# A recurrence split by token halves: its first half in steps beside the projections of the second half, the attention after them

## The chip, the cores and the metric

The kernel runs on one NeuronCore of a Trainium2 chip. TensorE (PE) does the matmuls, VectorE (DVE) and ScalarE (ACT) the elementwise work, GpSimd (POOL) a little of it; SyncE (SP) and POOL issue transfers. Each engine works through its own program in order, and they meet through semaphores. The metric is the device time of one execution in microseconds. The kernel before took 3598.67 us (median of three runs, 3595.58 to 3598.70).

## The reference, cut to what matters

Two transformer-like blocks over 1024 tokens of width 1024, in float32. The change lies in the mixer of the second block:

```python
h = _rmsnorm(x, mix_norm_gain[l])
proj = h @ w_in[l]
p_rwkv, p_attn = proj[..., :RWKV_COLS], proj[..., RWKV_COLS:]
y_rwkv = _rwkv7_mixer(p_rwkv, ...)
q, k, v = (t.reshape(B, S, ATTN_HEADS, HEAD_DIM) for t in jnp.split(p_attn, 3, axis=-1))
q = _partial_rotary(q, positions); k = _partial_rotary(k, positions)
o = _dilated_attention(q, k, v)
x = x + jnp.concatenate([y_rwkv, y_attn], axis=-1) @ w_out[l]
```

`_rwkv7_mixer` shifts each projection by a token, computes decay, gates and keys per token, and runs a recurrence of a 64x64 state over the tokens, eight heads wide:

```python
def step(state, inp):
    r_t, w_t, k_t, v_t, kk_t, a_t = inp
    sa = jnp.einsum('bhvk,bhk->bhv', state, -kk_t)
    state = (state * w_t[:, :, None, :]
             + sa[..., None] * (kk_t * a_t)[:, :, None, :]
             + v_t[..., None] * k_t[:, :, None, :])
    y = jnp.einsum('bhvk,bhk->bhv', state, r_t)
    return state, y
```

The attention has eight heads of width 64 too; each query sees earlier keys through three dilated windows.

## The kernel before, in words

Matmuls of weights are done three times (high by high, high by low, low by high part of the float32 numbers): `dense` (line 297) runs one weight tile of 128 output channels, 8 slices of the inner dimension, 24 matmuls of 512 columns for one half of the tokens. ACT makes the high part `w_hi` of a weight tile, DVE the low part `w_lo`, two tiles ahead (`next_tile`).

**Projections of block two** (`in3_*`, from line 1954). 26 tiles in the list `IN3` for the first 512 tokens, then the same 26 for the last 512: `wa2` and `gd2` (low-rank inputs of decay, a and gate), 12 `rkv`, 12 `aqkv` (the attention's q, k, v). ACT copies each result from PSUM, DVE does the token shift (two instructions, "mix") or the rotary turn (three), and SP writes the tile to DRAM (`K.rkv`, `K.attn`).

**Heads.** Then three streams share the engines: two of the recurrence (`rwkv_*`, g = 0 and 1) and the attention (`attention_*`). Each stream is a Python generator that yields at the end of a step; `braid` takes one step of each stream in turn, and writes them one behind the other into each engine's program. The second recurrence stream starts at step 20 (`LAG`). A recurrence stream has four units u (two pairs of heads j, two token halves hf), in the order `halves(g)`: (2g, 0), (2g, 1), (2g+1, 0), (2g+1, 1). Counting the yields, a unit has 56 steps for hf = 0 and 55 for hf = 1. In a unit: gates and decay (light on PE), products of 64x64 blocks, five levels of a triangular inverse (`Y`, then `X` and `Xt`, with a DVE step between), a chain `S` of up to 8 small steps for the state, and the norm. The attention has four blocks j of two heads, 40 steps each. In one there are 16 units (8 query blocks i by 2 heads): scores on PE, mask and maximum on DVE (`add_min`), exp on ACT, transposes on PE, copy on ACT, values on PE, copy on ACT; then a norm over the block. `half_over` makes each engine of a stream wait for the end of the stream's unit before.

All engines wait at `in3_over` before the heads: every tile of the projections is done and written. When the heads are over, the output projection `out2` (tiles `X2HA`, `X2LA`, ...) begins.

**Order of the work.** There is a second way of mixing here, used elsewhere in this kernel: a `Lane` keeps a list `bg` of generators, and `slots(n)` in the main program adds `fine` to an account for each slot and takes a step of the first generator when it has reached 1. A `dense` tile with one token half has 8 slots on PE, one behind each of its 8 slices (3 matmuls); DVE and ACT take the 8 slots in one go at the start of the tile, behind the split of a later weight and ahead of the wait for the tile's own result.

**Memory.** The streams use PSUM banks 0 and 1, 2 and 3 and (attention) 4 to 7; the projections use 0 to 3, the rotary turn 4 to 7. In the trace `r_...` are tiles of the recurrence (`r_in` its loaded r, k, v), `a_...` those of the attention, `XHB` and `XLB` the normalised input of the second token half, `over1hB` and `over1lB` the places that hold projected tiles until they are written.

## Time and profile before

| | |
|---|---|
| median of three runs | 3598.67 us (3595.58 to 3598.70) |
| the profiled execution | 3591.73 us, span 3589.9 us, granted clock 0.953 |
| PE busy over the span | 3265.2 us (91%) |
| DVE, ACT, POOL busy | 1751.6, 1188.3, 250.0 us (49%, 33%, 7%) |
| chain that ended last | PE 74%, DVE 15%, ACT 6%, issue 3% |
| second token half's projections | from 1928 to 2077 us |
| heads | from 2086 to 2758 us; `out2` from 2760.6 us |

"Granted clock" is the share of 2.4 GHz that the throttle gave TensorE on average over a stretch; it has two levels, 1.2 and 2.4 GHz. In the waits view a line says who waited for whom, the microseconds in total, the number of times and the longest. In the time-ordered view a row has its start, its length, engine, line, operation, output <- inputs, the number of instructions merged, and in brackets the idle time before it with what ended it.

### The profile page before, as it was taken

Reading aid. Unit: us, or ns where it says so; the run is one execution under the profiler, and the core shown is the slowest. Engines: PE = TensorE matmul, PEld = TensorE weight load, DVE = VectorE, ACT = ScalarE, POOL = GpSimd, SP = SyncE. Lnnn points to the kernel's source line nnn. Section 1 sums busy time; section 2 is a strip of 40 time slices with the busy share of each in tenths; the row PEclk is TensorE's granted clock in tenths of the full one; section 3 lists DMA queues with packets and bytes.
Section 4 is the critical chain, followed back from the end, with each engine's and each line's share of the span. In section 5 each row is a group of like instructions: output and inputs, shape, how many; then the busy total and the mean of one; then the engine's idle time right before and its main releaser. Section 6 shows DMA issues by size and latency. Waiting matters only on the chain.

```text
span 3589.9 us, 55150 instructions
## 1 busy us (share of the span) xinstructions
PE 3265.2 (91%) x23686; PEld 2733.8 (76%) x23686; DVE 1751.6 (49%) x2928; ACT 1188.3 (33%) x2050; POOL 250.0 (7%) x210
## 2 busy tenths in 40 slices
PE   5999878889989999998999978887877999999998
PEld 4887767768878888887777857675756878888887
DVE  6646343346574243436654444455555553333355
ACT  4231354452453221223433233433322431212133
POOL 1111010011130000001210000000001000000000
PEclk8999899999999999999999979898989999999999
DMA  2111121114332111123443410101001222111123
GB/s 100 67 65 48 63 81 66 69 58 141 135 108 90 55 42 53 40 77 102 140 150 135 156 52 20 37 2 36 2 19 60 94 96 69 47 47 49 48 93 111
DMA packets 86770, 262.28 MB, mean 73 GB/s; under 512 B 10208, under 2 KB 10336, under 8 KB 86400
## 3 DMA queue, kind: packets, MB, share of 16 engines
q1 hardware_dynamic: 76512, 224.07, 18.5%
q0 software_dynamic: 5120, 16.86, 1.3%
q10 hardware_dynamic: 4896, 17.84, 1.2%
q8 instruction: 187, 3.06, 0.4%
q14 instruction: 55, 0.45, 0.0%
HBM read 216.51 MB, written 42.21 MB: 72 GB/s over the span
## 4 chain that ended last, share of the span: by engine, by line
PE 74%; DVE 15%; ACT 6%; issue 3%; DMA 1%; POOL 1%; ACTq 0%; SPq 0%; DVEq 0%; POOLq 0%
PE ps L125 71%; PE ps L128 2%; DVE m_S L169 1%; DVE w_lo L159 1%; ACT w_hi L156 1%; ACT L138 1%; DVE r_t L159 1%; DVE HB L169 1%; PE ps L124 1%; DVE r_in L159 1%; DVE HB L159 1%; ACT m_D L138 1%; DVE r_Xa L159 1%; DVE r_t L169 0%; ACT r_t L138 0%
## 5 line engine op out<-in xcount | busy, mean ns | idle before, releaser
L159 DVE TENSOR_TENSOR w_lo<-w_raw,w_hi 128x1024 fp32r<-128x1024 f32 (+3 forms) x353 | 397.4, 1128 | 360.0 <-ACT w_hi L156 356.4
L125 PE MATMUL ps<-XHA,w_hi 128*128 128x264 f32 (+3 forms) x1456 | 476.4, 327 | 32.0 <-ACT m_G L138 8.8
L125 PE MATMUL ps<-XLA,w_hi 128*128 128x264 f32 (+3 forms) x1456 | 464.7, 319 | 0.0
L125 PE MATMUL ps<-XHA,w_lo 128*128 128x264 f32 (+3 forms) x1456 | 462.8, 318 | 0.0
L156 ACT ACTIVATE w_hi<-w_raw 128x1024 fp32r<-128x1024 f32 (+3 forms) x353 | 340.1, 964 | 348.0 <-PE ps L125 281.3
L125 PE MATMUL ps<-XHB,w_hi 128*128 128x512 f32 x920 | 369.2, 401 | 7.8 <-POOL XLB L159 5.7
L125 PE MATMUL ps<-XLB,w_hi 128*128 128x512 f32 x920 | 361.0, 392 | 0.0
L125 PE MATMUL ps<-XHB,w_lo 128*128 128x512 f32 x920 | 360.6, 392 | 0.0
L125 PEld LDWEIGHTS ps<-XHA,w_hi 128*128 128x128 f32 x1456 | 282.8, 194 | 64.5 <-issue 25.5
L125 PEld LDWEIGHTS ps<-XLA,w_hi 128*128 128x128 f32 x1456 | 283.3, 195 | 21.8 <-issue 4.1
L125 PEld LDWEIGHTS ps<-XHA,w_lo 128*128 128x128 f32 x1456 | 283.3, 195 | 16.7
L125 PEld LDWEIGHTS ps<-XHB,w_hi 128*128 128x128 f32 x920 | 174.5, 190 | 50.0 <-issue 9.3
L125 PEld LDWEIGHTS ps<-XLB,w_hi 128*128 128x128 f32 x920 | 174.4, 190 | 37.8 <-issue 3.1
L125 PEld LDWEIGHTS ps<-XHB,w_lo 128*128 128x128 f32 x920 | 174.1, 189 | 37.1
L159 DVE TENSOR_TENSOR HB<-HB,ps 128x512 f32<-128x512 f32 (+1 forms) x136 | 88.2, 655 | 217.8 <-PE ps L125 217.5
L125 PE MATMUL ps<-X2HA,w_hi 128*128 128x512 f32 x416 | 164.3, 395 | 9.3 <-DVE X2LA L159 5.2
L125 PE MATMUL ps<-X2LA,w_hi 128*128 128x512 f32 x416 | 163.5, 393 | 0.0
L125 PE MATMUL ps<-X2HA,w_lo 128*128 128x512 f32 x416 | 163.2, 392 | 0.0
L125 PE MATMUL ps<-X2HB,w_hi 128*128 128x512 f32 x416 | 162.7, 391 | 0.0
L125 PE MATMUL ps<-X2HB,w_lo 128*128 128x512 f32 x416 | 161.9, 389 | 0.0
L125 PE MATMUL ps<-X2LB,w_hi 128*128 128x512 f32 x416 | 161.8, 389 | 0.0
L166 DVE TENSOR_SCALAR C<-G,vecs 128x512 f32<-128x512 f32 x88 | 51.0, 579 | 214.8 <-ACT G L156 214.8
(445 smaller groups left out, 6244.7 us busy)
## 6 DMA issues: line engine op xcount, KB each, us to landing
w_raw<-in_f_gate SPq DMA_DIRECT2D x66, 512.0 KB, 3.2
w_raw<-in_f_up SPq DMA_DIRECT2D x66, 512.0 KB, 3.2
w_raw<-in_w_out SPq DMA_DIRECT2D x32, 512.0 KB, 3.2
w_raw<-in_f_down SPq DMA_DIRECT2D x48, 320.0 KB, 2.9
w_raw<-in_f_down SPq DMA_DIRECT2D x32, 384.0 KB, 3.1
w_raw<-in_w_rkv SPq DMA_DIRECT2D x24, 512.0 KB, 3.3
w_raw<-in_w_attn SPq DMA_DIRECT2D x24, 512.0 KB, 3.3
w_raw<-in_w_qkvo SPq DMA_DIRECT2D x16, 512.0 KB, 3.3
```

Source lines behind the costliest of these rows:

```text
L124: return Issued(e.matmul(out, a, b, start=start, stop=stop, skip_group_check=True))
L125: return Issued(e.matmul(out, a, b, start=start, stop=stop))
L128: return Issued(self.eng and self.eng.transpose(out, src, ident))
L138: return Issued(self.eng and self.eng.activation(out, src, func, **kw))
L156: return Issued(self.eng and self.eng.activation(out, src, ACT.Copy))
L159: return Issued(self.eng and self.eng.tensor_tensor(out, a, b, op))
L166: return Issued(self.eng.tensor_scalar(out, a, s1, s2, op0, op1))
L169: return Issued(self.eng and self.eng.scalar_tensor_tensor(out=out, in0=a, scalar=s, in1=b, op0=op0, op1=op1))
```

## The change

The order of a stream's units becomes (2g, 0), (2g+1, 0), (2g+1, 1), (2g, 1), so that the first two units of each stream need the first token half alone. The two recurrence streams begin with the first tile of the second token half's projections (`BEGIN`), in the background list, with `fine` = 0.55: 26 tiles x 8 slots x 0.55 give 114 steps there, of which the first 6 (`BEG`) are empty. What is left of them is run with the attention (`heads_rest`), which joins the braid when the projections are over and begins with two empty steps (`ATT`).

What goes with it: the state after the first half of a stream's first unit is kept aside (`D.kept`, one DVE copy) until its last unit; the second half's projections use PSUM banks 4 and 5, their rotary turn 6 and 7; their spill buffers and the low-rank inputs move into parts of `HB`; the loads `r_in<-rkv` move from SP's queue to POOL's, which has its own order of the two streams (`rwkv_load` in `rwkv_pool`); SP's queue holds the loads of the attention alone after the projections, and the first attention block's load, before issued while the projections ran (`LATER`), now comes behind `in3_over`; PE waits before `BEGIN` until DVE has read the last rotary result. The rotary turn of a tile stands one tile later in DVE's text, behind a further weight split.

```diff
+BESIDE, BEG, ATT = 0.55, 6, 2
...
-        b = K.fg.take(P, (name, m, c))
+        b = (ring or K.fg).take(P, (name, m, c))
...
-EARLY, LATER = (1, "rkv", 6), (1, "aqkv", 8)
+EARLY, BEGIN = (0, "aqkv", 4), (1, "wa2", 0)
...
+def banks3(K, c):
+    return K.fh if c else K.fg
...
+def lora_place(K, c, rows):
+
+    if c:
+        return K.HB[rows, 0 if rows.stop <= 64 else 2, 512:1024]
+    return K.HB[rows, 4 if rows.stop <= 64 else 5, 0:512]
...
     for c, name, i in IN3:
-        dense(P, K, S, name, i, 8, K.X, ready, [WIDE3[c]], [c])
+        if (c, name, i) == BEGIN:
+            P.wait_ge(S.dve, ("rot", 0, 10))
+            heads_begin(P, K, rwkv_pe)
+        dense(P, K, S, name, i, 8, K.X, ready, [WIDE3[c]], [c], banks3(K, c))
...
+        if t == BEGIN:
+            heads_begin(A, K, rwkv_act)
...
+            V.tt(K.ident2[:, :], K.ident[:, 0:64], K.ident[:, 64:128], ADD).then_inc(K.c.dve, "ident2")
+            heads_begin(V, K, rwkv_dve)
...
-            D.dma(K.amask[:, :], K.I["a_mask"]).then_inc(K.a_mask, by=16)
-            for g in range(2):
-                for n in range(3):
-                    at = SPILL3[0, "rkv", 6 * g + n]
-                    D.wait_ge(K.pst[at % 4], ("out", at))
-                rwkv_load(D, K, g, 0)
-        if t == LATER:
-            for n in range(3):
-                at = SPILL3[1, "aqkv", n]
-                D.wait_ge(K.pst[at % 4], ("out", at))
-            attention_load(D, K, 0)
...
-    return [(2 * g, 0), (2 * g, 1), (2 * g + 1, 0), (2 * g + 1, 1)]
+
+    return [(2 * g, 0), (2 * g + 1, 0), (2 * g + 1, 1), (2 * g, 1)]
+
+
+def first_half_over(L, K):
+
+    n3_over(L, K)
+    for sig in K.hs:
+        L.wait_ge(sig, ("h2", 1))
+    L.wait_ge(K.in3.pe, ("aqkv", 11, 0))
+    L.wait_ge(K.in3.act, ("aqkv", 0, 11))
+    L.wait_ge(K.in3.dve, ("turned", 0, 10))
+    for n in range(20, 24):
+        L.wait_ge(K.pst[n % 4], ("out", n))
...
+    yield from pause(BEG)
+    P.wait_ge(K.in3.act, ("aqkv", 0, 11))
...
+        elif u == 2:
+            V.vcopy(x.S0[:, 0:64], x.S0[:, 512:576]).then_inc(d, ("S", u, 0))
         else:
-            V.vcopy(x.S0[:, 0:64], x.S0[:, 512:576]).then_inc(d, ("S", u, 0))
+            V.vcopy(a16(x.S0[:, 0:64]), D.kept).then_inc(d, ("S", u, 0))
...
+        if u == 0:
+            V.after(d)
+            V.vcopy(D.kept, a16(x.S0[:, 512:576])).then_inc(d)
...
+        if u == 3:
+            V.wait_ge(K.rws[1 - g].pe, ("g", 3) if g else ("a", 3))
...
+        if u:
+            rwkv_load(G, K, g, u)
...
 def rwkv_load(D, K, g, u):
     T, (j, hf) = K.rw[g], halves(g)[u]
     for n in range(3):
+        at = SPILL3[hf, "rkv", 3 * j + n]
+        D.wait_ge(K.pst[at % 4], ("out", at))
+    for n in range(3):
         D.dma(T.in3[:, n, :], K.rkv[4 * n + j][:, 512 * hf:512 * hf + 512]).then_inc(T.ld, ("in", u), by=16)
-
-
-def rwkv_sp(D, K, g):
-    T, S = K.rw[g], K.rws[g]
-    for u in range(4):
-        half_over(D, S, u, None)
-        if u:
-            rwkv_load(D, K, g, u)
-        yield from pause(58)
...
 def attention_sp(D, K):
     S = K.at
+    in3_over(D, K)
+    D.dma(K.amask[:, :], K.I["a_mask"]).then_inc(K.a_mask, by=16)
     for j in range(4):
         if j:
+            D.wait_ge(K.a_ld, ("in", j - 1))
             D.wait_ge(S.pe, ("w", j - 1, 15))
-            attention_load(D, K, j)
-        yield
-        yield
-        yield from pause(34)
-        yield from pause(2 + Q5)
-        yield
+        attention_load(D, K, j)
 
 
...
 def attention_pe(P, K):
     S, ps = K.at, K.atb
+    yield from pause(ATT)
+    in3_over(P, K)
...
+        yield
+
+
+def heads_begin(L, K, rwkv):
+
+    L.drain()
+    L.streams = [rwkv(L, K, 0), rwkv(L, K, 1)]
+    L.bg.append(braid(L.streams))
+    L.fine = BESIDE
+
+
+def heads_rest(L, attention):
+
+    L.streams.append(attention)
+    L.drain()
+    L.fine = 0
 
 
 def heads_pe(P, K):
-    in3_over(P, K)
-    braid([rwkv_pe(P, K, 0), rwkv_pe(P, K, 1), attention_pe(P, K)])
+    heads_rest(P, attention_pe(P, K))
...
+    for g in range(2):
+        rwkv_load(G, K, g, 0)
+    first_half_over(G, K)
+    G.bg.append(braid([rwkv_pool(G, K, 0), rwkv_pool(G, K, 1)]))
+    G.drain()
 
 
 def heads_sp(D, K):
-    in3_over(D, K)
-    braid([rwkv_sp(D, K, 0), rwkv_sp(D, K, 1), attention_sp(D, K)])
+    attention_sp(D, K)
...
+    K.fh, K.sr = Banks(ps[4:6]), Banks(ps[6:8])
...
+        K.pS2 = [K.HB[:, 6 + n // 2, 512 * (n % 2):512 * (n % 2) + 512] for n in range(4)]
...
     in3_pe(P, K)
-    P.drain()
-    P.fine = 0
     heads_pe(P, K)
```

Three places in the order of the instructions. **PE, in a tile of the second token half's projections.** Before, the tile's matmuls stand next to each other, with a rotary matmul (`over1lB,cst`) between two tiles:

```order
L125 MATMUL ps<-XHB,w_lo 128x512
L125 MATMUL ps<-over1lB,cst 128x512
L125 MATMUL ps<-XHB,w_hi 128x512
L125 MATMUL ps<-XLB,w_hi 128x512
L125 MATMUL ps<-XHB,w_lo 128x512
```

Now, with stream 0 in its state chain (`r_S,r_Xa`) and stream 1 in a level of its inverse (`r_Xa,r_GB`):

```order
L127 MATMUL ps<-XHB,w_hi 128x512
L127 MATMUL ps<-XLB,w_hi 128x512
L127 MATMUL ps<-XHB,w_lo 128x512
L127 MATMUL ps<-r_S,r_Xa 64x64 x2
L127 MATMUL ps<-XHB,w_hi 128x512
L127 MATMUL ps<-XLB,w_hi 128x512
L127 MATMUL ps<-XHB,w_lo 128x512
L127 MATMUL ps<-r_S,r_Xa 64x64 x2
L127 MATMUL ps<-r_Xa,r_GB 64x64 x16
```

One slice or two of the tile stand between two steps of the recurrence. Of the recurrence's 4016 matmuls in the program, 1814 now stand among the tiles, and 2202 behind the last tile.

**DVE, over a tile in the same place.** Before, a weight split, two instructions of token shift, the next split:

```order
L159 TENSOR_TENSOR w_lo<-w_raw,w_hi 128x1024
L159 TENSOR_TENSOR over1hB<-over1hB 128x512
L169 SCALAR_TENSOR_TENSOR over1hB<-over1hB,vecs 128x512
L159 TENSOR_TENSOR w_lo<-w_raw,w_hi 128x1024
L159 TENSOR_TENSOR over1hB<-over1hB 128x512
```

Now the shift (`HB<-p_G`, then `HB<-HB,vecs,p_G`) and the split stand together, and the steps behind them until the next tile's:

```order
L161 TENSOR_TENSOR r_Xa<-r_Xa,ps 128x512
L161 TENSOR_TENSOR r_in<-r_in,ps 128x512
L161 TENSOR_TENSOR HB<-p_G 128x512
L171 SCALAR_TENSOR_TENSOR HB<-HB,vecs,p_G 128x512
L161 TENSOR_TENSOR w_lo<-w_raw,w_hi 128x1024
L161 TENSOR_TENSOR r_S<-ps,r_t 128x64
L161 TENSOR_TENSOR r_t<-ps,cst 128x512
L161 TENSOR_TENSOR r_S<-ps,r_t 128x64 x2
```

So three DVE instructions of a tile, the first of which waits for the tile's end on PE and its copy on ACT, stand between two steps of the recurrence.

**PE, at the end of the heads.** Before, the recurrence is last, and the output projection follows its last matmul:

```order
L125 MATMUL ps<-r_t,r_S 64x64
L125 MATMUL ps<-r_t,cst 128x512 x2
L125 MATMUL ps<-r_GD,r_gl 128x512
L125 MATMUL ps<-X2HA,w_hi 128x512
L125 MATMUL ps<-X2LA,w_hi 128x512
```

Now the recurrence's last matmul (`HB,r_gl`) stands early in the attention's last block:

```order
L127 MATMUL ps<-a_k,a_q 128x384 x2
L127 MATMUL ps<-HB,r_gl 128x512
L130 MATMUL ps<-cst,a_A 128x128 x3
L127 MATMUL ps<-a_VT,a_PT 128x64 x2
L130 MATMUL ps<-cst,a_A 128x128 x3
L127 MATMUL ps<-a_VT,a_PT 128x64 x3
L127 MATMUL ps<-a_k,a_q 128x512 x2
```

Behind it stand 68 of that block's 72 value matmuls (`a_VT,a_PT`), its norm, and then `out2`, with nothing of another stream between them.

## Rows read from the trace of the kernel before

**Rows 1.** Busy time by stretch; first line names the columns.
```profile
core 0: us, PE busy (x) PEld busy (x) DVE busy (x) ACT busy (x) POOL busy (x), PEclk, DMA share, GB/s
1928.00:2077.00 149.00, 149.00 (x642) 120.19 (x640) 65.97 (x79) 48.72 (x73) 0.00 (x0) 1.00 0.46 162
...
2086.00:2760.00 674.00, 546.50 (x9152) 449.44 (x9150) 338.38 (x665) 223.59 (x481) 25.70 (x16) 0.88 0.05 16
2592.00:2732.00 140.00, 107.45 (x2268) 87.78 (x2263) 71.62 (x122) 30.50 (x48) 6.67 (x4) 0.88 0.04 13
```

**Rows 2.** Waits, 2592 to 2732: us, times, longest.
```profile
PE ps L125 <- DVE r_in L159: 13.0, 9, 3.6
```

**Rows 3.** PE in order of time: stream starts, ends of attention blocks, next stage.
```profile
2085.65 2.07 PE L125 MATMUL ps<-r_WA,r_wl 32*128 32x512 f32 x4 [8.46 <-issue]
...
2204.33 1.09 PE L128 MATMUL ps<-cst,HB 128*128 128x128 f32 x8
...
2589.84 1.84 PE L128 MATMUL ps<-cst,HB 128*128 128x128 f32 x8
...
2760.57 0.77 PE L125 MATMUL ps<-X2HA,w_hi 128*128 128x512 f32 x1 [5.23 <-DVE X2LA L159]
```

**Rows 4.** DVE in order of time, 2730 to 2760: the two streams' last results.
```profile
2732.41 0.68 DVE L159 TENSOR_TENSOR HB<-r_t,ps 128x512 f32<-128x512 f32 x1
...
2757.94 0.69 DVE L159 TENSOR_TENSOR HB<-r_t,ps 128x512 f32<-128x512 f32 x1
```

**Rows 5.** PE groups that belong to the attention, 2086 to 2760.
```profile
L125 PE MATMUL ps<-a_VT,a_PT 128*128 128x64 f32 x576 | 76.4, 281 | 0.3 <-ACT HB L156 0.2
...
L128 PE MATMUL ps<-cst,a_A 128*128 128x128 f32 x320 | 55.1, 306 | 1.8 <-ACT a_A L138 1.7
...
L125 PE MATMUL ps<-a_k,a_q 64*128 64x512 f32 (+3 forms) x192 | 42.8, 551 | 6.7 <-ACT HB L156 6.7
...
L128 PE MATMUL ps<-cst,HB 128*128 128x128 f32 x32 | 6.4, 365 | 0.0
```

**Rows 6.** Busy time in two stretches where other recurrences run beside projections.
```profile
90.00:315.00 225.00, 209.56 (x1853) 185.80 (x1852) 128.00 (x389) 60.35 (x93) 40.68 (x12) 0.96 0.18 65
495.00:720.00 225.00, 193.38 (x1129) 161.71 (x1130) 76.09 (x152) 101.83 (x175) 1.02 (x6) 0.94 0.21 77
```

**Rows 7.** Groups on DVE and ACT while the second half is projected.
```profile
L159 DVE TENSOR_TENSOR w_lo<-w_raw,w_hi 128x1024 fp32r<-128x1024 f32 x26 | 31.4, 1219 | 4.0 <-ACT w_hi L156 4.0
...
L156 ACT ACTIVATE over1hB<-ps 128x512 f32<-128x512 f32 x20 | 12.0, 600 | 68.5 <-PE ps L125 68.5
...
L169 DVE SCALAR_TENSOR_TENSOR over1hB<-over1hB,vecs 128x512 f32<-128x512 f32 x9 | 6.8, 752 | 0.3
```

**Rows 8.** The attention's last pair and norm, in order of time.
```profile
2560.57 1.99 PE L125 MATMUL ps<-a_k,a_q 64*128 64x512 f32 x8 [0.41 <-ACT HB L156]
...
2563.00 0.75 DVE L173 CUSTOM_DVE_ANT_0 a_A<-a_mask,ps,a_mx 128x512 f32<-128x512 f32 x1 [0.50 <-PE ps L125]
...
2563.79 1.15 ACT L138 ACTIVATE a_A<-a_A,a_mx 128x1024 f32<-128x1024 f32 x1 [3.37 <-DVE a_mx L173]
...
2573.03 1.09 PE L128 MATMUL ps<-cst,a_A 128*128 128x128 f32 x8
...
2576.05 2.00 PE L125 MATMUL ps<-a_VT,a_PT 128*128 128x64 f32 x16
...
2580.17 1.22 DVE L159 TENSOR_TENSOR HB<-HB,a_den 128x1024 f32<-128x1024 f32 x1
...
2591.73 1.41 DVE L165 TENSOR_SCALAR HB<-ps,vecs 128x512 f32<-128x512 f32 x2 [1.08 <-PE ps L128]
```

**Rows 9.** Busy time in the first 42 us of the heads stage.
```profile
2086.00:2128.00 42.00, 34.98 (x312) 24.68 (x312) 18.45 (x39) 19.79 (x48) 2.95 (x2) 0.63 0.00 1
```

**Rows 10.** DMA issues: KB each, median us to landing.
```profile
r_in<-rkv SPq DMA_DIRECT2D x24, 256.0 KB, 3.5
...
mg<-mo POOLq DMA_DIRECT2D x8, 256.0 KB, 2.9
```

More of the change, by code:

```diff
@@ L294, in next_tile, with dense @@
     return i
-def dense(P, K, S, name, m, kt, X, ready, chunks, ids=None):
+def dense(P, K, S, name, m, kt, X, ready, chunks, ids=None, ring=None):
     i = next_tile(P, K, None)
@@ L2001, in in3_act @@
                 A.cp(s, b).then_inc(S.act, ("aqkv", c, i))
-            K.fg.done((name, i, c), S.act, ("aqkv", c, i))
+            ring.done((name, i, c), S.act, ("aqkv", c, i))
             continue
         n, place = SHIFT3[t], PLACE3[name, i]
-        G = K.pG[n % 2]
+        G = pairs3(K, c)[n % 2]
         if n >= 2:
@@ L2293, in rwkv_act @@
     a = S.act
+    yield from pause(BEG)
+    first_half_over(A, K)
     for u, (j, hf) in enumerate(halves(g)):
@@ L2383, in rwkv_dve @@
     level = lambda n: K.levels[:, n, :].unsqueeze(1).broadcast_to([128, 8, 64])
+    a16 = lambda s: s.rearrange("p (a x) -> p a x", x=16)
+    yield from pause(BEG)
+    first_half_over(V, K)
+    V.wait_ge(K.c.dve, "ident2")
     for u, (j, hf) in enumerate(halves(g)):
@@ L2646, in attention_act @@
     a = S.act
+    yield from pause(ATT)
+    in3_over(A, K)
     for j in range(4):
+        for g in range(2 if j < 2 else 0):
+            A.wait_ge(K.rws[g].pe, ("g", 1) if j else ("a", 1))
         yield
@@ L2705, in attention_dve @@
     d = S.dve
+    yield from pause(ATT)
+    in3_over(V, K)
     for j in range(4):
@@ L2992, in make_memory @@
     sb = scope(xs)
-    K.X = Split([sb("XHA", [128, 8, 528], R), sb("XHB", [128, 8, 512], R)], [sb("XLA", [128, 8, 528], R), sb("XLB", [128, 8, 512], R)], 528)
+    XHA, XLA = [sb(n, [128, 8, 528], R) for n in ("XHA", "XLA")]
+    XHB, XLB = [sb(n, [128, 8, 512], R) for n in ("XHB", "XLB")]
+    K.X = Split([XHA, XHB], [XLA, XLB], 528)
     K.pn.X = K.X
```

129 lines of the change are left out of this document (64 added, 65 removed).

## The prediction, made before the changed kernel was run

> **What bounds the kernel now.** I read the busy times by stretch first. While the second token half is projected, from 1928 to 2077 us, PE is busy without a gap at the full clock, 149.0 us; in the heads, from 2086 to 2760 us, it is busy 546.5 of 674 us at a granted clock of 0.88 [rows 1]. So 128 us of PE time lie idle there, and some are worked at half clock, while the stage ahead has no idle time at all. The change lays the one beside the other.
>
> The order of time then gives the pace of the steps, which is what I build the sum on. The streams start at 2085.65 us, and the attention's four blocks of 40 steps end near 2204.33 and 2589.84 us (first and last of four) [rows 3]. With all three streams that makes 385.5 us for 120 steps, **3.2 us a step**. From 2592 to 2732 us only the two recurrence streams run, for the 62 steps from step 160 to the end of stream 0 at step 222: 140 us, **2.26 us a step**, of which PE is busy 107.5/62 = 1.73 us at clock 0.88 [rows 1, 4]. The last 20 steps have stream 1 alone, near its unit's end: 2757.94 - 2732.41 = 25.5 us, **1.28 us a step** [rows 4]. The difference 3.2 - 2.26 = **0.94 us** is what the attention adds to a step. Where PE waits with two streams, it is most of all for DVE between two levels of the inverse, 13.0 us in 9 waits, the longest 3.6 us [rows 2].
>
> The stretch that the change remakes runs from 1928.13 us (the first tile of the second half, at the edge of the stretch in [rows 1]) to 2760.57 us [rows 3], **832.4 us**: 149 of projections, 9 of a gap (8.46 us idle [rows 3]) and 674 of heads.
>
> **Part by part: the tiles with the recurrence beside them.** The tiles cost 149 us of PE. The recurrence's PE time in the heads is 546.5 less the attention's 76.4 + 55.1 + 42.8 + 6.4 = 180.7 [rows 1, 5], so 365.8 us at clock 0.88; at full clock 322. Of its 4016 matmuls 1814 move, 45%: 145 us. With no idle time at all the mixed stretch is 149 + 145 = 294 us (314 if the recurrence's matmuls stay at the mean clock of the heads). If the tiles filled nothing, it would be the steps at their own pace and the tiles on top: 94 steps with both streams x 2.26 + 14 with stream 0 alone x 1.28 + 149 = 379 us. These are the two ends. Between two steps stand 1.8 slices of a tile, 149/114 = 1.3 us of PE work, against 2.26 - 1.73 = 0.53 us of idle time per step, so most of the small waits are covered. Not covered is what DVE does at the end of each tile: two shift instructions (0.75 us for the second, and I take the same for the first) and the split of 1.22, which begin only when PE has ended the tile and ACT has copied it, 0.60 [rows 7]: with the handoffs 3.6 us in which DVE serves no step. PE has a first step ready and 1.3 us of tile on each side of it, so I expect it to lose 0.5 to 1.5 us of the 3.6, on 26 tiles. The nearest rows for the whole are the two stretches in which this kernel already runs a recurrence beside weight tiles: PE is idle there 225 - 209.6 = 15.4 us (7%) and 31.6 us (14%) [rows 6]. I take the middle, 10.5%: 294/0.895 = 328.5 us, and 1.5 us for PE's new wait for DVE ahead of the first tile, behind which the whole of PE's program stands: **330 us**. The same shares give 316 and 342; the 14% on 314 gives 365.
>
> **The rest with the attention.** Stream 0 has 229 steps in all and stream 1 248, of which 114 are done. Left are 115 steps with both and the attention, x 3.2 = **368 us**, and 19 with stream 1's end and the attention, x (1.28 + 0.94) = **42 us**. Both come from the same steps before; the blocks of the attention are the same, and PE's clock should be too. I give them 10 us either way.
>
> **The attention alone.** It has 162 steps and so 28 more, with 68 of the last block's 72 value matmuls behind the recurrence's last matmul: query blocks 2 to 7, their norm, and nothing beside them. The trace of before never shows it alone, since the recurrence always outlasted it. From the rows of its last pair, two units over eight key blocks: scores 1.99 us, two transposes of 1.09, two value groups of 2.00 = 8.2 us, 1.02 us per key block [rows 8]. Blocks 2 to 7 have 33 of them: 34 us of PE. Per pair PE then waits from the last scores through mask (0.75), exp (1.15, with its accumulator read of 0.19) and the handoffs, 2.6 us at the end and 2 at the start: 14 us for six. The norm goes from 2580.17 to the end of the output scaling at 2593.1 [rows 8], 13 us with others between; its own operations are 9.5. Sum 57.5 at full clock. What the clock does there is the unknown: at 1.2 GHz the 34 us double, 91.5. I take **68 us**, nearer the fast end, because the last pair itself ran at full clock in the trace (1.09 us for 8 transposes; the first 42 us of the stage had 0.63 [rows 9]). The Trainium skill, TensorE: Matmul & The Clock Gate, section HAM oscillation, says that a PE that keeps pausing between short bursts is throttled again each time; by that the term would be 91.5 and the whole 24 us later. The first 42 us of the heads, which follow a gap and have light work, agree with it [rows 9]; the stage as a whole, at 0.88, does not [rows 1].
>
> **The gaps.** Before, 8.5 us between the last tile and the heads. Now two steps of the recurrence run, and then every engine waits in its own queue at `in3_over`, with the recurrence's steps behind it, for the last tile's turn and write; and the attention's first load, which was issued early, comes behind that, with q, k and v of 512 KB. Some 12 us of chain against 4 steps of cover: **6 us**, 0 to 12. From the last result to `out2` 3 us, as now (2757.94 to 2760.57 [rows 3, 4]).
>
> **Edits at nothing.** The two copies of the state are a 128x64 DVE copy each. The loads of r, k, v go from SP's queue to POOL's: 3 transfers per unit, six units; POOL's landed in 2.9 us for 256 KB, SP's in 3.5 [rows 10], and the lora matmuls and sigmoids stand ahead of them in each unit. The Trainium skill, DMA: Bandwidth & Descriptors, section Specifications, has the GpSimd path slower to its first byte, about 1 against 0.6 us; by that each unit would start 0.4 us later, 2.4 us in all if nothing hid it. The landing times here show no such loss. If POOL's order put a load late, a unit would start some us late, 6 times; I keep 5 us for it in the range.
>
> **Sum.** 330 + 368 + 42 + 68 + 6 + 3 = 817 us against 832.4: **15.4 us less**. The profiled execution would go from 3591.73 to 3576.3 us; the median of the runs lies 6.9 us above that execution, so I forecast 3598.67 - 15.4 = **3583 us**. No change means within 0.2%, 7.2 us; the forecast is two of these below.
>
> **The rivals.**
> *The tiles fill it all.* The mixed stretch at the 7% idle share, and the attention alone at 58 us: 316 + 368 + 42 + 58 + 3 + 3 = 790, 42 less: 3556 us. For it: 1.3 us of tile per step against 0.53 us idle. Against: DVE's 3.6 us at each tile's end have no counterpart in the stretch with 7%.
> *DVE's tile work stalls the steps* (slower than before). The place is the end of each of the 26 tiles; the price is what PE loses of the 3.6 us beyond its first step. At 2.4 us a tile the mixed stretch is 294 + 62 = 356, and the sum 843, +11: 3610 us; with no filling at all (379) it is 866, 3632 us. It decides from a mixed stretch of 345.6 us, 2 us lost per tile. For it: the longest waits of two streams are of this size already [rows 2]. Against: DVE is to be busy at most 66 + 0.45 x 338 = 218 of 330 us [rows 1].
> *The attention alone at half clock.* 91.5 us, sum 841, +8: 3607 us; with half of this effect it is 3595, no change. It is also the case in which the Trainium skill's rule holds.
> *The change does not do what it says*: the steps run to the end of the tiles without overlap, because PE waits at each for the engine that is behind; that is the 379 us above, and I count it there.
>
> **How the numbers follow.** Forecast case 0.45, own range 3567 to 3600; all filled 0.19; DVE stall 0.22; half clock 0.14. Faster by more than 0.2%: 0.34 of the first, 0.19 of the second, 0.01 of the rest = 0.54. Within: 0.10 + 0.04 + 0.05 = 0.19. Slower: 0.01 + 0.17 + 0.09 = 0.27. The range goes from 3546 (all filled, the load and gap terms at their best) to 3622 (half of the way between the DVE case and no filling).
>
> **What would show it.** In the changed profile: the stretch of the `XHB` tiles is 310 to 345 us long with PE 86 to 94% busy at a clock above 0.95; the waits of PE there are for DVE tiles `r_in`, `r_t`, `r_S`, under 2 us each. Behind it a step goes on at 3.2 us, four attention blocks near 128 us each up to the last. The last 65 us or so have only `a_...` tiles on PE, with waits for ACT's exp. A mixed stretch over 346 us, or an attention end over 85 us, makes me wrong.

## The result, and the profile after

| | before | after |
|---|---|---|
| median | 3598.68 us (3595.58 to 3599.05, 4 runs) | 3619.93 us (3615.30 to 3620.88, 4 runs) |
| ratio, 95% interval | | 1.0058 (1.0041 to 1.0076) |
| profiled execution, span | 3591.73, 3589.9 us | 3615.3, 3613.5 us |

The change makes the kernel slower by 21 us; I had forecast 15 us faster. Outside the remade stretch nothing moved: the tiles of the second half begin at 1928.3 us (before 1928.13), and from the first `X2HA` matmul to the end it is 829.3 us in both. The stretch itself went from 832.4 to **855.9 us**; the prediction had 817. Stretches and rows come from the profiled execution of each kernel, medians from all of them; one execution lies up to 12 us off its kernel's median.

Busy time by stretch of the kernel after, in the columns of [rows 1]: the mixed stretch, the gap, the heads up to the recurrence's end, the attention alone.

```profile
core 0: us, PE busy (x) PEld busy (x) DVE busy (x) ACT busy (x) POOL busy (x), PEclk, DMA share, GB/s
1928.30:2284.00 355.70, 324.55 (x4267) 246.23 (x4268) 184.74 (x278) 96.55 (x150) 15.43 (x14) 0.96 0.19 62
2284.00:2302.00 18.00, 8.42 (x119) 5.48 (x118) 6.49 (x10) 3.00 (x5) 0.00 (x0) 0.77 0.49 175
2302.00:2712.00 410.00, 335.82 (x5169) 271.48 (x5168) 197.28 (x416) 148.61 (x341) 20.39 (x20) 0.89 0.06 21
2712.00:2784.00 72.00, 51.08 (x239) 41.85 (x239) 18.20 (x44) 24.69 (x60) 0.13 (x1) 0.60 0.01 1
```

The mixed stretch has 31 us of idle time (8.8%), less than I had allowed, but 324.6 us of work, where I had 294. In the gap PE is busy 8.4 of 18 us. The attention alone runs at a granted clock of 0.60, that is mostly at 1.2 GHz. At 355.7 us the mixed stretch is over the 346 that I had named as a sign of being wrong.

PE in order of time answers to [rows 3]: the wait for the end of the projections, the wait for the attention's load, the first and the last attention block's norm, the next stage.

```profile
2294.63 1.97 PE L127 MATMUL ps<-r_AM,r_in 64*64 64x128 f32 x16 [4.43 <-issue]
2301.75 1.54 PE L130 MATMUL ps<-cst,a_A 128*128 128x128 f32 x6 [5.15 <-DMA a_A<-attn]
...
2434.29 1.09 PE L130 MATMUL ps<-cst,HB 128*128 128x128 f32 x8
...
2779.03 1.97 PE L130 MATMUL ps<-cst,HB 128*128 128x128 f32 x8 [6.22 <-DVE HB L161]
2784.16 0.77 PE L127 MATMUL ps<-X2HA,w_hi 128*128 128x512 f32 x1 [3.16 <-DVE X2LA L161]
```

DVE answers to [rows 4]: stream 0's last result, then stream 1's, 44.0 us later. From there it is 73.7 us to the next stage, in which only the attention works.

```profile
2666.55 0.69 DVE L161 TENSOR_TENSOR HB<-r_t,ps 128x512 f32<-128x512 f32 x1 [1.39 <-PE ps L127]
...
2710.51 0.69 DVE L161 TENSOR_TENSOR HB<-r_t,ps 128x512 f32<-128x512 f32 x1 [0.46 <-PE ps L127]
```

What PE waits for in the mixed stretch, answering to [rows 2]:

```profile
PE ps L127 <- DVE r_in L161: 12.5, 6, 6.4
PE ps L127 <- DVE r_t L161: 8.9, 5, 6.0
```

The longest are 6 us, where I had expected under 2. The attention's groups, the first of them here, answering to [rows 5] (76.4 us there), cost PE more than before; the last block ran mostly at 1.2 GHz:

```profile
L127 PE MATMUL ps<-a_VT,a_PT 128*128 128x64 f32 x576 | 84.9, 302 | 0.0
```

The loads answer to [rows 10]: 3.2 us for the six that are issued beside the tiles, 3.7 over all 24, against 3.5 from SP's queue. None of PE, DVE and ACT has a wait for them in the stretch, so their move to POOL's queue cost nothing that shows.

```profile
r_in<-rkv POOLq DMA_DIRECT2D x6, 256.0 KB, 3.2
```

### The profile page after: what moved, and what is told of

The parts are those of the page before. It is cut to its first block, busy times and chain, and to the rows that moved or that the text cites. A ratio compares the mean times of both kernels' runs of the same rounds, so it can differ in the third digit from the quotient of the medians.

```text
span 3613.5 us, 55140 instructions
## 1 busy us (share of the span) xinstructions
PE 3288.6 (91%) x23686; PEld 2728.5 (76%) x23686; DVE 1752.1 (48%) x2930; ACT 1190.2 (33%) x2051; POOL 263.1 (7%) x234
## 4 chain that ended last, share of the span: by engine, by line
PE 73%; DVE 15%; ACT 7%; issue 3%; DMA 2%; POOL 1%; ACTq 0%; SPq 0%; DVEq 0%; POOLq 0%
PE ps L127 70%; PE ps L130 2%; DVE w_lo L161 2%; DVE m_S L171 1%; ACT L140 1%; ACT w_hi L158 1%; DVE HB L171 1%; DVE HB L161 1%; PE ps L126 1%; DVE r_t L161 1%; DVE a_A L175 1%; DVE r_in L161 1%; ACT m_D L140 1%; ACT r_t L140 0%; DVE r_Xa L161 0%
## 5 line engine op out<-in xcount | busy, mean ns | idle before, releaser
L127 PE MATMUL ps<-XHB,w_hi 128*128 128x512 f32 x920 | 383.9, 417 | 9.2 <-POOL XLB L161 6.1
```

The source lines that it names most:

```text
L127: return Issued(e.matmul(out, a, b, start=start, stop=stop))
```

## The experiments

All of them edit the changed kernel. "Stretch" is from the first `XHB` matmul to the first `X2HA` matmul, "mixed" its part up to the end of the last tile, "behind" the rest.

### How many steps to move

The pace `BESIDE` is 0.55 in the changed kernel. A smaller one needs an edit beside it: ACT's attention waits for the last reader of the first half's low-rank inputs in `HB`, and that reader would come too late. Two copies on ACT take the inputs to a new place, from which the recurrence then reads them.

```diff
-BESIDE, BEG, ATT = 0.55, 6, 2
+BESIDE, BEG, ATT = 0.4, 6, 2      # and 1e-9, 0.2, 0.3, 0.38, 0.42, 0.45
...
-    return K.HB[rows, 4 if rows.stop <= 64 else 5, 0:512]
+    return K.HB[rows, 1 if rows.stop <= 64 else 3, 512:1024]
...
+            A.cp(lora_place(K, 0, slice(0, 64)), K.HB[0:64, 4, 0:512]).then_inc(S.act, ("wa", 0))
+            A.cp(lora_place(K, 0, slice(0, 96)), K.HB[0:96, 5, 0:512]).then_inc(S.act, ("gd", 0))
...
-        for g in range(2 if j < 2 else 0):
-            A.wait_ge(K.rws[g].pe, ("g", 1) if j else ("a", 1))
```

No steps moved: 

> No step of the recurrence runs beside the second half's projections; units, loads, late attention load and the rest are as in the changed kernel, and two copies on ACT move the low-rank inputs of the first half out of the attention's way. Theory 'a price that depends on how many are moved' (each moved step costs 1.8 us of the mixed stretch and saves 2.26 at the end, but once the attention has nothing left beside it each further moved step leaves one attention step alone): within 6 us of the time before (3593 to 3605), the attention outlasted by the recurrence, no stretch with the attention alone. Rival 'the other edits cost' (queue order of the loads, late load of the attention, copies): 3612 us or more.

0.2: 

> As the run without steps beside the tiles, with a fifth of the first units' steps beside them (the pace table at 0.2 for 0.55). Price by number: 0.45 us gained for each moved step, some 40 steps: about 17 us less than the run without them, 3587 us, mixed stretch about 225 us. Rival 'each moved step costs more beside the tiles than it saves' (TensorE's switching and VectorE's tile work): the time rises evenly with the number moved, some 7 us above the run without them.

0.4: 

> The pace table at 0.4. Price by number: some 80 steps moved, 0.45 us each, and the attention's 160 steps are just covered by the recurrence's: 30 to 36 us less than the run without moved steps (3570 to 3587 us), and no stretch of the attention alone longer than 20 us. Rival 'each moved step costs': 12 to 15 us above the run without them, near the changed kernel's time.

Later, to find out what the copies cost, where the time turns, and whether 0.4 was luck:

> The changed kernel at its own pace 0.55, with the two copies of the low-rank inputs that the runs at other paces have. If they cost nothing to speak of: the ratio to the kernel before within 0.15% of the changed kernel's 1.0058, stretch 854 to 859 us. If they cost what separates the paces: stretch over 870 us, or under 840.

> Pace 0.45, 10 steps more beside the tiles than at 0.4, where the attention and the recurrence end together. Theory 'a step is worth 2 us only while the recurrence outlasts the attention, and at most 1.4 us beyond, at 2.65 us beside the tiles': mixed stretch 300 us (27 more), behind it 8 to 14 us less, so 13 to 19 us more than at 0.4: 3567 to 3577 us. Rival 'the turn comes later': 3550 to 3558 us.

> Pace 0.30: 866 of the recurrence's matmuls beside the tiles. From the runs at 0.20 and 0.40: mixed stretch 148 + 866 x 0.098 + 7 idle = 240 us, behind it the recurrence outlasts the attention by 195 matmuls, 575 to 585 us. If the time depends on the number alone, the stretch is 806 to 814 us, and the time 3565 to 3573 us. If 0.40 is a lucky phase, this run's mixed stretch has 20 us or more of idle time and the time is 3580 us or more.

> Pace 0.38: 1080 matmuls beside the tiles, 3 left behind the attention. Number alone: 3553 to 3562 us, idle time in the mixed stretch 10 to 14 us. Lucky phase: idle time 20 us or more, and 3566 us or more.

> Pace 0.42: 1189 matmuls beside the tiles, nothing of the recurrence left behind the attention. Number alone (8 us more in the mixed stretch, 3 less behind it): 3557 to 3566 us. Idle time that rises with the pace whenever VectorE comes late (28 us at 0.45): half of that rise already, 3565 to 3575 us. Lucky phase: as much as at 0.45, 3580 us or more.

Measured (us; "moved" counts the recurrence's matmuls in the program ahead of the last tile, of 4016; each has two records in the trace, which the x counts of the rows count; "PE busy" is that of the mixed stretch, "clock" the granted clock behind it):

| pace | moved | mixed | PE busy | idle | behind | clock | stretch | median | ratio, 95% |
|---|---|---|---|---|---|---|---|---|---|
| 0 | 0 | 148.1 | 148.1 | 0 | 703.7 | 0.86 | 851.8 | 3616.42 | 1.0058 (1.0043, 1.0073) |
| 0.2 | 416 | 189.6 | 188.1 | 1.5 | 630.9 | 0.86 | 820.5 | 3582.38 | 0.9968 (0.9955, 0.9981) |
| 0.3 | 866 | 246.3 | 232.9 | 13.4 | 571.5 | 0.89 | 817.8 | 3574.78 | 0.9945 (0.9928, 0.9961) |
| 0.38 | 1080 | 264.1 | 253.8 | 10.3 | 532.6 | 0.90 | 796.7 | 3558.44 | 0.9899 (0.9884, 0.9914) |
| **0.4** | 1124 | 273.2 | 261.4 | 11.8 | 523.7 | 0.90 | 796.9 | **3555.78** | **0.9895 (0.988, 0.991)** |
| 0.42 | 1189 | 290.5 | 271.8 | 18.7 | 508.3 | 0.91 | 798.8 | 3561.99 | 0.9912 (0.9894, 0.9929) |
| 0.45 | 1350 | 316.6 | 288.1 | 28.5 | 516.0 | 0.88 | 832.6 | 3592.02 | 0.9989 (0.9979, 0.9998) |
| 0.55, copies | 1814 | 358.4 | 325.1 | 33.3 | 506.9 | 0.83 | 865.3 | 3623.94 | 1.0079 (1.0064, 1.0094) |
| 0.55, changed kernel | 1814 | 355.7 | 324.6 | 31.1 | 500.2 | 0.84 | 855.9 | 3619.93 | 1.0058 (1.0041, 1.0076) |

Busy time by stretch at 0.4 (mixed, gap, rest), and DVE's last two results there:

```profile
1928.50:2201.70 273.20, 261.35 (x2886) 197.26 (x2886) 144.60 (x214) 84.09 (x132) 13.15 (x12) 0.99 0.23 79
2201.70:2220.80 19.10, 10.74 (x196) 8.11 (x196) 12.01 (x20) 2.57 (x4) 0.00 (x0) 0.76 0.51 181
2220.80:2725.40 504.60, 415.77 (x6710) 343.93 (x6711) 249.28 (x515) 182.87 (x419) 22.30 (x23) 0.90 0.05 18
```

```profile
2719.44 1.41 DVE L167 TENSOR_SCALAR HB<-ps,vecs 128x512 f32<-128x512 f32 x2 [3.87 <-PE ps L130]
2722.79 0.69 DVE L161 TENSOR_TENSOR HB<-r_t,ps 128x512 f32<-128x512 f32 x1
```

They are the attention's last result and the recurrence's last: at 0.4 they end within 3 us of each other. What follows:

- Moving steps does gain. From pace 0 to 0.4 the stretch loses 55 us. The PE time of a moved matmul beside the tiles hardly changes: 40.0 us for 416, 113.3 for 1124, 176.5 for 1814, that is 0.096, 0.101 and 0.097 us (0.104 at 0.42 and 0.45). Its worth behind them is not. Up to 0.4 "behind" shrinks by 180 us, 0.160 us a matmul; from 0.4 to 0.55 by 17 us with the copies in both, 0.024 us.
- The reason is who comes last. Behind the gap the attention's 162 steps take 504.6 us at 0.4 and 489.2 at 0.55 with the copies (2304.7 to 2793.9), though 690 matmuls of the recurrence are gone. Steps taken from beside the attention are nearly free where they stand, and cost 0.12 us a matmul beside the tiles, waits included. Only those that stood behind its end are worth moving.
- What "behind" is made of can be read from the records, by the reckoning that stands in the part on why the prediction was wrong. From 0 to 0.4 it loses 96 us of PE work (as it would be at full clock), 32 us that the half clock had cost, and 52 us of idle time. From 0.4 to 0.55 with the copies it loses 48 us of work, but the half clock costs 24 us more again and idle time grows by 7. So the worth of a step falls for two reasons that come together: the attention now ends last, and TensorE, with less to do beside the attention, works longer at 1.2 GHz, 176 us instead of 108.
- 0.4 and its two neighbours lie on one floor, 797 to 799 us, so it is no lucky phase. Between 0.42 and 0.45 there is a step of 34 us: 16 are the work of 161 more matmuls, 10 idle time in the mixed stretch (below), and 8 stand behind it. There the trace has the attention alone, with the way to `out2`, for 19.4 us at 0.45 and for 4.6 at 0.42, and a granted clock of 0.88 against 0.91; no run separates the two.
- With no step moved the other edits cost 19 us against the kernel before: the first rival was right there, and my expectation of 3593 to 3605 us missed. So did those at 0.2 and 0.4, which came out 5 us under 3587 and 14 under the range, since I had priced a step at 0.45 us; that at 0.3, by 2 us over; and that at 0.45, where both of its ranges lay 15 us and more too low. Those at 0.38 and 0.42 held. The copies cost 9 us of the stretch at 0.55, between the two values I had named.

### Where the idle time comes from

At 0.45 and 0.55 PE's idle time is three times that at 0.38. The first of its two long pieces in the kernel after (the other, 6.41 us, ends at 1998.72), with DVE ahead of it:

```profile
1948.81 2.05 PE L127 MATMUL ps<-r_t,cst 128*128 128x512 f32 x2 [6.00 <-DVE r_t L161]
```

```profile
1943.20 0.69 DVE L161 TENSOR_TENSOR HB<-p_G 96x512 f32<-96x512 f32 x1 [1.48 <-ACT p_G L158]
1943.93 0.75 DVE L171 SCALAR_TENSOR_TENSOR HB<-HB,vecs,p_G 96x512 f32<-96x512 f32 x1
1946.32 1.23 DVE L161 TENSOR_TENSOR w_lo<-w_raw,w_hi 128x1024 fp32r<-128x1024 f32 x1 [1.64 <-ACT w_hi L158]
...
1947.97 0.69 DVE L161 TENSOR_TENSOR r_t<-r_t 128x512 f32<-128x512 f32 x1
```

This is the place that the prediction named: DVE does the tile's shift and the weight split first, waits twice for ACT in between, and only then serves the step for which PE waits. What ACT did meanwhile:

```profile
1938.60 1.28 ACT L140 ACT_TABLE_LOAD   x1 [0.56 <-PE ps L127]
...
1941.18 1.28 ACT L145 ACT_TABLE_LOAD   x1
1942.48 0.60 ACT L158 ACTIVATE p_G<-ps 128x512 f32<-128x512 f32 x1
...
1943.19 1.28 ACT L140 ACT_TABLE_LOAD   x1
1944.71 0.63 ACT L140 ACTIVATE HB<-HB 96x512 f32<-96x512 f32 x1 [0.24 <-DVE HB L171]
1945.24 1.04 ACT L158 ACTIVATE w_hi<-w_raw 128x1024 fp32r<-128x1024 f32 x1
1946.30 1.28 ACT L140 ACT_TABLE_LOAD   x1
...
1951.52 1.28 ACT L140 ACT_TABLE_LOAD   x1
```

ACT takes the tile's sigmoid between two functions of the recurrence, and loads a table at each change: five in 14 us here. One of them (1943.19) stands ahead of the sigmoid and so of `w_hi`, for which DVE's split waited. The Trainium skill, ScalarE: Activation LUTs, section What ACT_TABLE_LOAD costs, gives 1283 ns for one; the trace agrees, to the nanosecond. In the same first stretch (1928 to 2250 us) the group at L140 has 8 loads at 0.45 and in the kernel after, and 5 at 0.42 and at 0.4, which this row is from:

```profile
L140 ACT ACT_TABLE_LOAD x5 | 6.4, 1283 | 12.1 <-PE ps L127 12.1
```

So three more loads come with the step between 0.42 and 0.45. How much of it they make is not shown: no run changes them alone.

### Is it the switching, or the waits?

```diff
-            while self.due >= 1:
-                self.due -= 1
-                self.step()
+            if self.due >= self.lump:
+                while self.due >= 1:
+                    self.due -= 1
+                    self.step()
```

`lump` is 2 for PE alone: 

> The changed kernel with TensorE taking its steps beside the tiles two at a time, so that it changes half as often between tile slices and steps; VectorE's and ACT's order is untouched. Theory 'switching costs TensorE 0.18 us a step': 57 changes fewer, the mixed stretch 10 us shorter (346 us, PE busy about 315) and 3610 us. Rival 'VectorE's waits are what counts': two steps in a row wait for VectorE between them as in a stretch with two streams, idle time in the mixed stretch grows by 0.3 to 0.5 us a pair, and the time stays or rises (3615 to 3640 us).

Measured: 3624.04 us (3611.62 to 3629.55), ratio 1.0088 (1.0071, 1.0105). Mixed 358.0 us:

```profile
1928.70:2286.70 358.00, 320.45 (x4267) 253.07 (x4268) 183.72 (x278) 96.17 (x149) 15.44 (x14) 0.94 0.18 62
```

PE's work fell by 4.1 us, against the kernel after, and its idle time rose by 6.4 to 37.5. But the clock was not the same: 41 us of this stretch ran at 1.2 GHz, 27 in the kernel after (granted 0.94 against 0.96). With both reckoned at full clock (an estimate; how it is made stands in the part on why the prediction was wrong) PE's work fell by 9.7 us, which is what the switching theory had; the half clock took 5.6 of them back, and the longer waits more than the rest. The time lies where the rival had it, in 3615 to 3640 us.

Changes priced by themselves, with matmuls that nobody waits for or reads:

```diff
+    def extra(self, n):            # called for PE's slots; lump 1, or 8 = once a tile
+        self.cnt += n; self.owed += 0.55 * n
+        if self.cnt % lump == 0:
+            while self.owed >= 1:
+                self.owed -= 1
+                ...                # 16 matmuls ident[0:64, 0:64] x itself
```

One group behind each slice: 

> Price of switching by itself. As the run without moved steps, but with 16 matmuls of 64x64 that nothing waits for and nothing reads, behind each of the slices behind which the changed kernel has a step: 114 groups of 16 among the 26 tiles. The tiles alone are 148 us. Theory 'switching costs 0.2 us a group': this run's tile stretch is 20 us or more longer than that of the run with the same 1824 matmuls in 26 lumps at the tiles' ends. Rival 'a group's start and end cost nothing to speak of': the two differ by less than 6 us.

Lumps: 

> As the last, with the 1824 matmuls in 26 lumps of about 70, one at each tile's end: 88 changes between tile and small matmuls fewer. Switching theory: tile stretch 148 + 1824 times the matmul's own spacing (0.075 to 0.11 us, by the recurrence's 1.73 us for 17) = 285 to 350 us, and 20 us under the other. Rival: the same within 6 us.

```profile
1931.20:2334.60 403.40, 403.33 (x4288) 332.06 (x4288) 65.53 (x79) 45.52 (x71) 0.00 (x0) 1.00 0.15 51
```

```profile
1932.60:2303.40 370.80, 370.78 (x4288) 332.68 (x4288) 65.48 (x78) 46.13 (x71) 0.00 (x0) 1.00 0.17 55
```

114 groups took 403.4 us, 26 lumps 370.8, both at full clock and without idle time: 32.6 us for 88 changes there and back, **0.37 us a change**. So changing between tile slices and small matmuls has a price, and the lumps came out 21 us above the top of what I had named for them (350). The recurrence's real groups pay less: in `b2` 41 groups fewer stand among the tiles' records (53 for 94), and 9.7 us are 0.24 us for each. Why these are cheaper is not shown.

Where the price stands can be read from the tiles' own matmuls: the first one of a slice, `XHB,w_hi`, takes longer, the two behind it hardly. First the run with no step moved, then 114 groups, then the kernel after:

```profile
L127 PE MATMUL ps<-XHB,w_hi 128*128 128x512 f32 x208 | 84.1, 404 | 0.8 <-DVE over1lB L161 0.8
L141 PE MATMUL ps<-XHB,w_hi 128*128 128x512 f32 x208 | 96.5, 464 | 0.8 <-DVE over1lB L175 0.8
L127 PE MATMUL ps<-XHB,w_hi 128*128 128x512 f32 x208 | 99.4, 478 | 0.8 <-DVE over1lB L161 0.8
```

### The overlap with the tiles, without the attention

```diff
-    heads_rest(P, attention_pe(P, K))
+    heads_rest(P, only_over(P, K))     # pause(ATT), in3_over; ACT and DVE alike; SP: in3_over
```

> No attention at all (its operations and its load are left out), no step beside the tiles: the recurrence by itself. The paces of the profile before (20 steps with stream 0 alone at 1.28, 209 with both at 2.26, 19 with stream 1 alone at 1.28) make 522 us, with 12 to 18 us between the last tile and the first step: from the first tile to the next projection 149 + 537 = 686 us. If the attention's running beside it costs the recurrence little, it is over 640; if both compete for TensorE, less than 690.

> No attention at all, 114 steps beside the tiles as in the changed kernel. This prices the overlap with tiles by itself. Theory 'the tiles fill idle time, 0.45 us a step': 356 + 8 + 115 x 2.26 + 19 x 1.28 = 648 us from the first tile to the next projection, 30 to 50 us less than the run without attention and without moved steps. Rival 'switching and VectorE's tile work eat the filling': the two are within 10 us, and all that moving steps brings comes from the attention's being covered elsewhere.

Measured: stretches of 677.5 and 653.5 us, from one execution each. First no steps moved (tiles, gap, recurrence alone), then 114.

```profile
1932.60:2080.30 147.70, 147.66 (x638) 119.77 (x639) 65.55 (x78) 45.62 (x70) 0.00 (x0) 1.00 0.42 135
2080.30:2089.30 9.00, 1.23 (x4) 0.36 (x2) 1.98 (x3) 0.60 (x1) 0.00 (x0) 0.83 0.40 134
2089.30:2610.10 520.80, 388.90 (x8033) 320.53 (x8033) 264.03 (x447) 112.56 (x179) 37.42 (x35) 0.85 0.04 11
```

```profile
1932.60:2287.90 355.30, 324.17 (x4266) 245.70 (x4267) 184.88 (x278) 97.77 (x151) 15.45 (x14) 0.96 0.20 62
2287.90:2586.10 298.20, 222.83 (x4409) 179.49 (x4407) 145.80 (x250) 63.83 (x102) 20.56 (x21) 0.84 0.05 16
```

The recurrence alone takes 520.8 us; the paces of before had said 522. Its PE work is 388.9 us at clock 0.85. Moving 114 steps costs 207.6 us beside the tiles and saves 231.6 (9.0 + 520.8 - 298.2): **24 us in all, 0.21 us a step**, under the 30 to 50 of my theory and over the 10 of the rival. With one execution each this is a rough number: executions of one kernel above differ by up to 18 us in all. The attention plays no part in the mixed stretch, which is the same 355 us.

One more, with `lump` 4 on the second of these: 

> No attention; 114 steps beside the tiles, TensorE taking four at a time. With one at a time the tile stretch was 355 us, TensorE busy 324 of it, so 176 us for the moved steps, as much as their share (45%) of the recurrence alone at clock 0.85. Theory 'changing between slices and steps costs what the clock gives back': a quarter of the changes, so busy goes down by 85 x 0.12 to 0.37 us = 10 to 31 us (293 to 314), while the idle time grows by as much or more. Rival 'the moved matmuls take their time whatever the clock': busy stays at 320 to 326.

```profile
1924.80:2308.80 384.00, 324.61 (x4267) 263.43 (x4268) 183.90 (x278) 97.14 (x151) 15.40 (x14) 0.91 0.18 58
```

PE's work stays at 324.6 us; idle time goes from 31 to 59 us, and the stretch from 653.5 to 684.0 us, more than with no step moved. By the total the rival was right, the moved matmuls take their time whatever the clock. The records say otherwise: 72 us of the mixed stretch ran at 1.2 GHz instead of 27, and at full clock PE's work would have been 299.6 us instead of 315.1. So 66 groups fewer saved 15.5 us, 0.23 each, and the half clock cost just as much more. Spreading the steps is worth 30 us, one execution against another.

### The attention's tail

Every sixth step of the attention joined to the one before:

```diff
+def hurried(s):
+    n = 0
+    for _ in s:
+        n += 1
+        if n % 6:
+            yield
-    L.streams.append(attention)
+    L.streams.append(hurried(attention))
```

> The changed kernel (pace 0.55, with the two copies of the low-rank inputs) in which every sixth step of the attention joins the one before, on all engines, so that its 162 steps pass beside 135 of the recurrence's. Theory 'the loss is the attention left alone': the 72 us alone at the end go down to under 15 us, the 27 steps cost some 0.9 us each beside the recurrence, and the whole comes to 3560 to 3580 us, level with the run at 0.4 or better. Rival 'the moved steps themselves are too dear at 0.55' (a mixed stretch of 356 us for steps worth less): the heads get no shorter than the 25 us that the tail's halved clock costs, and the time stays above 3595 us.

Measured: 3597.25 us (3583.77 to 3601.41), ratio 1.0004 (0.9993, 1.0014). The tail is gone, and the stretch is 836.4 us, 29 less than at 0.55 with the copies; but it is 39.5 more than at 0.4. The rival was right (its border was 3595 us): 82 us more in the mixed stretch bring 43 behind it, even with both streams ending together, at 2763.5 and 2766.4 us. The loss at 0.55 has then two parts: 29 us the tail, 39.5 moved steps that are worth too little.

A clock test, with one unread matmul more per step of the attention once it is alone:

```diff
+        if len(P.streams) == 1:
...
+                P.mm(b[:, 0:512], K.gl[0:96, 0:128], K.gl[0:96, 0:512], True, True)
```

> The changed kernel with one more matmul (96x512 in plain fp32, its result unread) on TensorE in each of the attention's last 28 steps, where nothing else runs beside them. Theory 'the tail is long because of the clock' (72 us at 0.60 granted): with TensorE kept busy the granted clock rises to over 0.9 and the stretch alone falls to 55 to 62 us though TensorE has 17 us more to do. Rival 'the tail is a chain through VectorE and ACT': the clock may rise, but the stretch stays at 70 us or grows, up to 90.

```profile
2713.70:2777.30 63.60, 56.95 (x306) 37.16 (x304) 19.38 (x47) 25.56 (x63) 0.30 (x1) 1.00 0.01 3
```

The clock goes from 0.60 to 1.00, and the tail from 73.7 to 63.6 us, though PE does 58 matmul records (28 us) more; my range was 55 to 62. At least ten us of the tail were the clock, since the added matmuls may stand in the way too. This is one execution, but the tail without them is 73.7 and 74.5 us in the two kernels at 0.55. The Trainium skill, TensorE: Matmul & The Clock Gate, section HAM oscillation, has a PE with repeated pauses throttled again and again; the trace agrees, 0.60 without the extra work and 1.00 with it.

### The gap and the start

> As the run without moved steps, but with the recurrence's pause before its first step cut from 6 steps to 1, and the attention's raised from 2 to 3. The run without moved steps was 19 us longer than the kernel before between the first tile and the next projection (851.8 against 832.4). Theory 'the recurrence starts 5 steps late': those cost 5 x 2.3 = 11 us and come back: 838 to 843 us for the stretch. Rival 'the loads in POOL's queue and the late load of the attention': the first step waits for them all the same, 849 us or more.

(`BEG` 1 for 6, `ATT` 3 for 2.) Measured: stretch 844.7 us, 7 less than 851.8, between the two values I had named and not more than executions of one kernel differ by. If it holds, the recurrence's late start is some of the 19 us. Another 3.5 stand in the gap, where PE in this run is idle for 6.8 us and then, for the attention's load, 5.1, against 8.5 before [rows 3]:

```profile
2096.71 1.97 PE L130 MATMUL ps<-cst,a_A 128*128 128x128 f32 x8 [5.13 <-DMA a_A<-attn]
```

> Pace 0.35 instead of 0.4, and the attention begins 7 steps behind the last tile instead of 2, so that five more steps of the recurrence stand ahead of the engines' wait for the end of the tiles and the attention's load. Theory 'the 10 us gap is open idle time that steps can fill': 10 fewer steps in the mixed stretch (20 us shorter), 10 more behind it of which 5 run in the gap, the attention and the recurrence ending within a few steps of each other: 3545 to 3553 us, below the run at 0.4. Rival 'the gap is not on the path, since the attention needs its load anyway': 3556 to 3565 us.

Measured: 3568.02 us, ratio 0.9922 (0.9905, 0.9938), stretch 803.4 us. A miss, by 3 us above the rival even. Its pace lies between 0.3 (817.8 us) and 0.38 (796.7), and so does its stretch: steps put into the gap brought nothing that shows. Loading its tiles beside the projections, as the kernel before does, was not tried: in the new layout they overlap `XHB`, which the tiles still read.

## Why the prediction was wrong

**The step that failed** is the PE time of the mixed stretch, "149 + 145 = 294 us". Measured are 324.6, and the moved matmuls cost 176.5 (324.6 - 148.1) and not 145. The size of the recurrence's own work is nearly right. What I had put at nothing, without a reason, is what the change between tile slices and steps costs, and that part of this stretch runs at half clock.

How the 31 us divide can be worked out from the records of the stretch, as an estimate: each gets the busy time that it adds to those before it, and one at 1.2 GHz is reckoned with the mean of its form at full clock. The tiles' matmuls then take 160.2 us, where they took 142.1 with no step moved: **18 us for 94 groups of steps among them**, 0.19 us each, as at 0.2 (25 groups) and 0.4 (65). The half clock costs **9 us**: the trace has it in five pieces, 27.3 us in all, in which PE works 19.2. And the moved matmuls themselves take 148.7 us, **4 us** more than 145. The whole recurrence takes 339 us by this reckoning, before, after and alone, where I had 322: group sums overlap, so taking the attention's 180.7 us off took too much.

That the clock does count for these matmuls, the same group of records shows at half clock and at full, in the kernel after; so do the tiles' matmuls, which start 0.43 us after each other and then 0.23:

```profile
1998.72 1.98 PE L127 MATMUL ps<-r_Xa,r_GB 64*64 64x64 f32 x32 [6.41 <-DVE r_in L161]
2000.62 0.79 PE L127 MATMUL ps<-XHB,w_hi 128*128 128x512 f32 x1
2001.21 0.63 PE L127 MATMUL ps<-XLB,w_hi 128*128 128x512 f32 x1
2001.64 0.63 PE L127 MATMUL ps<-XHB,w_lo 128*128 128x512 f32 x1
...
2004.81 0.50 PE L127 MATMUL ps<-XHB,w_hi 128*128 128x512 f32 x1
2005.15 0.40 PE L127 MATMUL ps<-XLB,w_hi 128*128 128x512 f32 x1
2005.38 0.39 PE L127 MATMUL ps<-XHB,w_lo 128*128 128x512 f32 x1
...
2008.64 1.15 PE L127 MATMUL ps<-r_Xa,r_GB 64*64 64x64 f32 x32
```

Two of the half-clock pieces; each begins within one of the two waits of 6.0 and 6.4 us:

```profile
1945.40:1952.20 6.80, 3.39 (x6) 2.11 (x7) 2.32 (x3) 3.45 (x4) 0.00 (x0) 0.50 0.22 77
1996.60:2003.40 6.80, 4.68 (x57) 3.82 (x59) 4.14 (x8) 0.00 (x0) 0.00 (x0) 0.50 0.30 109
```

The recurrence alone costs 0.097 us a matmul at a clock of 0.85, and 0.097 again beside the tiles at 0.96. That looks as if the clock did nothing, and it is chance: alone the half clock makes up the difference to 0.084, beside the tiles mostly the changes do. The clocks of 0.96 and 0.94 in the two nearest stretches [rows 6] could have been read ahead; what a change costs could not, from the rows shown.

**The idle share** (10.5%) was right: 8.8%. My rival of VectorE's stalls gave 356 us for the mixed stretch too, and so came out at 3610, near the truth, but for another reason: PE lost 31 us there in all, not 62 on top of 294.

**Behind it** I had 487 us (6 + 368 + 42 + 68 + 3), and it took 500. The gap has 9.6 us of idle time instead of 6; stream 1's end 44.0 instead of 42; the attention alone with the way to `out2` 73.7 instead of 71. The rest of the 13 us is spread over the 115 steps. The attention alone stood between my value and the 91.5 of the half-clock rival, whose mechanism was right (0.60) and whose price was too high: the tail came out 18 us under it. The clock was worth at least 10 us, and part of the tail is waits for ACT and DVE, PE being busy for 51 of 72 us.

**What the sum hid** is why such a change can fail. I priced each moved step at the average of its stretch and let "the attention adds 0.94 to a step" stand. It is the other way round: beside the attention the recurrence is nearly free. The rows of before bound the gain: the attention's last norm stands at 2589.84 us, the next stage at 2760.57 [rows 3]. Only the 169 us between could be won. They hold 1280 of the recurrence's matmuls, and their PE work stands in the trace of before:

```profile
2591.40:2760.60 169.20, 124.67 (x2563) 100.98 (x2562) 81.33 (x141) 35.83 (x58) 6.99 (x5) 0.87 0.04 12
```

Beside the tiles 1280 matmuls cost about as much, at 0.097 us 124, and some 12 us of waits come to it: some 33 us are left, and at 0.4 it is 35.5 (832.4 - 796.9). Beyond that number each matmul costs and brings almost nothing. The 169 us and the 125 in them could be read ahead.

**The edits at nothing**: the loads on POOL's queue were free as priced. The other edits together were not: the run without moved steps is 19 us longer than before. The pause is perhaps 7 of them and the longer gap 3.5; what the new order of the units costs, and in that run the two copies, is not separated.

## What to carry to other kernels

When work is moved out of a stretch where several streams run, count it at what the stretch gets shorter, not at its pace: only the part that outlasts the other streams is worth its full time, so move just as much as makes all end together. Here that is a pace of 0.4: 3555.78 us, 1.05% faster than the kernel before, where 0.55 is 0.6% slower. For the work that is moved, add to its own time what each change between it and its new neighbours costs, here 0.2 us, and compare stretches at the same clock: two totals can agree only because a lower clock hides a saving.

## What I had not expected of the hardware

- Small matmuls follow the clock nearly as much as wide ones do: 32 records of 64x64 take 1.98 us at 1.2 GHz and 1.15 at 2.4. That two stretches at 0.85 and 0.96 came to the same 0.097 us a matmul says nothing about it.
- Taking half or three quarters of the changes away saved PE's work, but the waits grew and the granted clock fell: 72 us at half clock instead of 27 took back all of the 15.5 us.
- A change from 128x512 to 64x64 matmuls and back costs 0.37 us with nothing to wait for, in groups of 32 records; in the recurrence's own steps some 0.2.
- 28 us of useless matmuls made a stretch 10 us shorter: they brought its granted clock from 0.60 to 1.00.
